# Split halves at multiples of 1024 bytes: placement in SBUF of the operands of TensorE's three-product matmuls

## The chip, the cores and the metric

One core of a Trainium2 chip. The metric is the device time of one execution in microseconds (us), the median of several runs. A lower time is better.

## The reference

Two model blocks in a row on 256 tokens of width 1024, all in float32, for one sequence:

```python
# first block, two layers
for layer in range(DEPTH):
    h = rms_norm(x, g_mix[layer])
    qkv = h @ w_in[layer]
    ...
    mix = jnp.concatenate([o_a, o_b, o_c], axis=-1)
    x = x + mix @ w_out[layer]
    h2 = rms_norm(x, g_ffn[layer])
    x = x + conv_gated_mlp(h2, w_up[layer], conv_w[layer], conv_b[layer], w_down[layer]).astype(x.dtype)
return rms_norm(x, g_final)
# second block, one layer
    xn = rmsnorm(h, norm1_g[layer])
    proj = xn @ w_in[layer]
    ...
    h = h + merged @ w_out[layer]
    hn = rmsnorm(h, norm2_g[layer])
    h = h + peer_ffn(hn, peer_wq[layer], peer_k1[layer], peer_k2[layer], peer_u[layer], peer_v[layer])
```

`o_a`, `o_b` and `o_c` are three kinds of attention. The second block has a state-space branch and an attention on chosen keys. `peer_ffn` chooses 128 of 16384 experts for each token; the kernel computes the hidden value of every expert, multiplies it by a gate that is zero for those not chosen, and sums over all.

## The kernel before

**Units.** The weights come from HBM as units of 128 partitions x 1024 floats (512 KB each), in one fixed list, `plan`. A unit goes into a slot: unit i into slot i % 6 up to the end of `keys`, and from the experts' units on (`ut`, `vt`) into slot j % 4. A slot has three buffers of 1024 words a partition: `raw`, `wh` and `wl`. SyncE issues the load of a unit into `raw` as soon as the slot's last unit has been split.

**The split.** For most products float32 accuracy is had from three matmuls of a faster type (fp32r): ScalarE copies `raw` to `wh`, rounded (line 1112); VectorE (line 1461) or GpSimd (line 2117) writes the remainder, `raw` - `wh`, to `wl`; a table `lower` says who. The activations are split the same way: `hh` and `hl`, the normed tokens turned (8 slices of 256 columns each); `yTh` and `yTl`, the hidden values of the gated MLP (22 slices of 256 columns each); `ach` and `acl`, 256 columns of the experts' gated hidden values, two buffers each. The function `mm3` issues for each pair of slices high x high, high x low and low x high (line 542), all into one PSUM bank:

```python
for j, (a, b) in enumerate(((0, 0), (0, 1), (1, 0))):
    m = p.e.matmul(out, lhs[i][a], rhs[i][b], start=start and i == 0 and j == 0, stop=stop and i == n - 1 and j == 2)
```

The second argument is the stationary operand, always 128 columns here; the third one is the moving operand. The profile writes out<-moving,stationary.

**Stages, in the order of the program,** with the products of line 542 that a unit has:

| stage | units | matmuls per unit | moving | stationary |
|---|---|---|---|---|
| win, wout (both layers) | 24 + 8 each | 12 | 512 columns of `wh`/`wl` | 128 of `hh`/`hl` |
| wup (both layers) | 44 each | 24 | 256 of `hh`/`hl` | 128 of `wh`/`wl` |
| wdown (both layers) | 22 each | 12 | 512 of `wh`/`wl` | 128 of `yTh`/`yTl` |
| wout2 | 8 | 12 | 512 of `wh`/`wl` | 128 of `hh`/`hl` |
| wpq | 16 | 24 | 256 of `hh`/`hl` | 128 of `wh`/`wl` |
| ut (experts, up) | 128 | 24 | 256 of `hh`/`hl` | 128 of `wh`/`wl` |
| vt (experts, down) | 128 | 12 | 512 of `wh`/`wl` | 128 of `ach`/`acl` |

Between the two blocks' ends stand products in whole float32 (lines 597, 837, 967, 533), straight from `raw`, which are not split. In `ut`, from unit 59 on, each unit is followed by eight small products that make the gates of four tokens; VectorE makes their one-hot operands. Before, VectorE does the routing (the choice of experts) with buffers that are cut from the upper part of `H` by `RT`, from word `R_AT` on. `H` holds the hidden values, 256 words a unit; ScalarE writes unit j of it, and from the unit on that reaches into the routing's buffers it waits for the event selG (line 1415), VectorE's last copy of routing results.

**Placement.** Each tensor of SBUF is allocated by `scoped`, one behind the other in the order of the code; closing an `ExitStack` frees its part for what comes next. In the built program the first one, `xs`, begins at byte 16512 of a partition: 16384 bytes are kept as scratch for DMAs whose descriptors GpSimd writes, and 128 hold constants. From there on follow `xs` (8192 bytes), `ids` (512), `hh` and `hl` (8192 each; `hw` and `sel_s` use the same bytes at other times), `sta` (3040), then 4 buffers each of `raw`, `wh` and `wl` (4096 each), and so on. The sizes of `sta` (760 words), `con` (1612) and `sml` (788) are what they need.

Of the kernel before, what the change touches and what calls it, by code (L numbers as in the profile page):

```python
# [30 lines left out]
K_W = K_T + 256  # L31
# [8 lines left out]
S_W = S_AIM + 16  # L40
# [55 lines left out]
def program(nc, x_d, pos_d, consts_d, smalls_d, win_d, wout_d, wup_d, wdown_d, rows_d, wu_d, wqkv_d, wqk_d, wga_d, wsm_d,  # L96
            wglu_d, wsu_d, wau_d, wout2_d, wpq_d, keys_d, ut_d, vt_d, out_d, spill_d):
    with ExitStack() as ctx:

        def scoped(where, name, n, dt=F32):  # L100
            return where.enter_context(nc.sbuf_tensor(name, [128, n], dt))

        xs = scoped(ctx, "xs", 2048)
        ids = scoped(ctx, "ids", 128)

# [1 line left out]
        hh, hl = scoped(sc_h, "hh", 2048, F32R), scoped(sc_h, "hl", 2048, F32R)  # L107
        sc_h.close()
        hw, sel_s = scoped(ctx, "hw", 2048), scoped(ctx, "sel_s", 2048)
        sta = scoped(ctx, "sta", 760)  # L110
        raws = [scoped(ctx, f"raw{i}", 1024) for i in range(4)]
        whs = [scoped(ctx, f"wh{i}", 1024, F32R) for i in range(4)]
        wls = [scoped(ctx, f"wl{i}", 1024, F32R) for i in range(4)]
        early = ExitStack()
        con_s = scoped(early, "con", K_W - 128)
        sml_s = scoped(early, "sml", S_W)
        tab_s = scoped(early, "tab", 8192)
        raws += [scoped(early, f"raw{i}", 1024) for i in (4, 5)]
        whs += [scoped(early, f"wh{i}", 1024, F32R) for i in (4, 5)]
# [34 lines left out]
        def signal(name, step=1):  # L154
            return Signal(ctx.enter_context(nc.semaphore(name)), name, step)
# [4 lines left out]
        x0_in, x1_in, pos_in, id_in, con_in, sml_in, wsb_in, wsc_in, out_sent, spilled, back_in = [  # L160
            signal(n, 16) for n in ("x0_in", "x1_in", "pos_in", "id_in", "con_in", "sml_in", "wsb_in", "wsc_in", "out_sent", "spilled", "back_in")]
# [140 lines left out]
        def sml(c, n):  # L302
            return sml_s[:, c:c + n]
# [130 lines left out]


        H = H_s[:, :].rearrange("p (j t) -> p j t", j=128)
        R_AT = 16800
        assert R_AT >= K_W - 128 + S_W + 8192 + 6144
        r_at = [R_AT]

        def RT(n):
# [653 lines left out]
        def act(a):  # L1095
            def load(out, src, sig, ev):
                a.e.dma_start(out, src).then_inc(sig.up(ev), 16)
# [63 lines left out]
            for t in range(2):  # L1161
                squares(("n", 0), t, x[:, t, :], mix[:, t, :], 0, (x0_in, x1_in)[t], "x")
            stream_up_to(first["win", 0])
            load(con_s[:, :], consts_d[:, 128:K_W], con_in, "con")
            load(sml(0, S_W), smalls_d, sml_in, "sml")
            turned(("n", 0), (0, ), 2)
            stream_up_to(first["win", 0] + 1)
# [238 lines left out]
            for j in range(128):  # L1406
# [7 lines left out]
                a.wait_ge(pe_out, ("hid", j))  # L1414
                if j * 256 + 256 > R_AT:
                    a.wait_ge(dve_out, ("selG", 1))
# [838 lines left out]
        for engine in (pe, sp, act, dve, pool):  # L2255
            engine(Engine(Count(), True))
# [8 lines left out]
        @block.scalar  # L2265
        def _(e):
            act(Engine(e, False))
# [130 lines left out]
```

## Time and profile before

| | |
|---|---|
| time, median of 3 runs | 1750.53 us (1750.17 to 1751.01) |
| span of the profiled execution | 1747.2 us |
| matmuls | 10714 |
| PE busy (union of modelled durations) | 1691.7 us, 97% |
| DVE, ACT, POOL busy | 1149.2, 821.6, 706.5 us |
| HBM read | 279.33 MB, 161 GB/s over the span |

The page gives the profiled execution by its span alone. Times inside it are us from the span's start. PE is TensorE, DVE VectorE, ACT ScalarE, POOL GpSimd, SP SyncE. A matmul's duration in a row runs from its start to a modelled end, so the durations of neighbours overlap; starts are measured. The timeline rounds to 0.01 us, and so a distance between matmuls is best taken over a whole unit: 12 distances in a stage with 512 moving columns, 24 in one with 256, or 11 where a wait stands at the unit's border.

### The profile page before, as it was taken

To read this page: it belongs to the slowest core of one execution; us is meant where nothing else is said; L and a number is where in the kernel's file an instruction comes from. 1 tells how busy PE (TensorE), PEld (TensorE's weight loads), DVE (VectorE), ACT (ScalarE), POOL (GpSimd) and SP (SyncE) were. 2 spreads that over 40 slices of the span, in tenths; PEclk is the share of its full clock that TensorE was granted. 3 is DMA by queue.
4 is the path that set the end of the run, shared out by engine and by line. 5 is a ranking of instruction groups with operands and counts; after the bars stand their busy time and mean duration, and the time that the engine had idled before them with its cause. 6 is when DMAs were issued, how large, how long until landed. Compare 5 with 4: busy or idle time off the path is not lost.

```text
span 1747.2 us, 27224 instructions
## 1 busy us (share of the span) xinstructions
PE 1691.7 (97%) x10714; PEld 1454.8 (83%) x10714; DVE 1149.2 (66%) x2422; ACT 821.6 (47%) x1453; POOL 706.5 (40%) x384
## 2 busy tenths in 40 slices
PE   7999999999999998999999999999999999999997
PEld 6779998777799986544579999999999988888885
DVE  6655785756367576666332999999999644444443
ACT  5455665354476642113243554544444455555553
POOL 2424667132357721432163999700000144444443
PEclk9999999999999999999999999999999999999998
DMA  7333545463255564323353656544444566666664
GB/s 292 112 109 132 182 162 195 150 217 108 74 193 190 173 203 134 111 87 109 95 194 134 216 167 198 179 147 145 145 140 139 160 193 193 194 194 195 195 193 134
DMA packets 77455, 283.20 MB, mean 162 GB/s; under 512 B 8720, under 2 KB 8976, under 8 KB 77072
## 3 DMA queue, kind: packets, MB, share of 16 engines
q1 hardware_dynamic: 76032, 276.50, 48.8%
q10 hardware_dynamic: 1296, 4.97, 0.8%
q8 instruction: 85, 1.39, 0.3%
q14 instruction: 42, 0.34, 0.1%
HBM read 279.33 MB, written 2.10 MB: 161 GB/s over the span
## 4 chain that ended last, share of the span: by engine, by line
PE 78%; DVE 8%; ACT 5%; POOL 5%; issue 3%; DMA 1%; POOLq 0%; DVEq 0%; ACTq 0%
PE bank L542 62%; PE bank L533 7%; PE bank L597 5%; POOL wl L2117 4%; ACT wh L1112 2%; DVE att L1478 2%; PE bank L665 1%; DVE wl L1461 1%; ACT att L1115 1%; PE bank L967 1%; PE bank L889 1%; DVE ssb L1467 1%; DVE mix L1506 1%; DVE xs L1467 1%; PE bank L837 0%
## 5 line engine op out<-in xcount | busy, mean ns | idle before, releaser
L2117 POOL TENSOR_TENSOR wl<-raw,wh 128x1024 fp32r<-128x1024 f32 x213 | 548.0, 2584 | 699.6 <-ACT wh L1112 691.1
L542 PE MATMUL bank<-hh,wh 128*128 128x256 f32 x1856 | 526.2, 284 | 5.5 <-POOL wl L2117 4.8
L1112 ACT ACTIVATE wh<-raw 128x1024 fp32r<-128x1024 f32 x476 | 492.7, 1050 | 57.2 <-PE bank L542 40.8
L542 PE MATMUL bank<-hl,wh 128*128 128x256 f32 x1856 | 519.1, 280 | 0.0
L542 PE MATMUL bank<-hh,wl 128*128 128x256 f32 x1856 | 518.1, 279 | 0.0
L1461 DVE TENSOR_TENSOR wl<-raw,wh 128x1024 fp32r<-128x1024 f32 x263 | 352.8, 1347 | 98.7 <-ACT wh L1112 98.2
L542 PEld LDWEIGHTS bank<-hh,wh 128*128 128x128 f32 x1856 | 349.1, 188 | 7.0 <-POOL wl L2117 6.0
L542 PEld LDWEIGHTS bank<-hl,wh 128*128 128x128 f32 x1856 | 349.2, 188 | 0.0
L542 PEld LDWEIGHTS bank<-hh,wl 128*128 128x128 f32 x1856 | 349.0, 188 | 0.0
L1467 DVE TENSOR_TENSOR acl<-H,ach 128x256 fp32r<-128x256 f32 x128 | 87.5, 685 | 181.6 <-ACT ach L1115 181.6
L542 PE MATMUL bank<-wh,ach 128*128 128x512 f32 x512 | 199.3, 389 | 0.4 <-DVE acl L1467 0.4
L542 PE MATMUL bank<-wh,acl 128*128 128x512 f32 x512 | 199.2, 389 | 0.0
L542 PE MATMUL bank<-wl,ach 128*128 128x512 f32 x512 | 199.2, 389 | 0.0
L1115 ACT ACTIVATE H<-bank 128x256 f32<-128x256 f32 (+32 forms) x199 | 64.7, 325 | 240.6 <-PE bank L542 208.0
L1115 ACT ACTIVATE ach<-H 128x256 fp32r<-128x256 f32 x128 | 53.4, 418 | 172.7 <-PE bank L542 172.2
L542 PE MATMUL bank<-wh,hh 128*128 128x512 f32 x288 | 119.3, 414 | 5.5 <-DVE hl L1467 2.9
L1478 DVE SCALAR_TENSOR_TENSOR att<-bank,sml,att 128x255 f32<-128x255 f32 (+1 forms) x176 | 84.4, 480 | 56.7 <-ACT att L1115 53.5
L542 PE MATMUL bank<-wh,hl 128*128 128x512 f32 x288 | 114.1, 396 | 0.0
L542 PE MATMUL bank<-wl,hh 128*128 128x512 f32 x288 | 113.9, 396 | 0.0
L542 PEld LDWEIGHTS bank<-wh,ach 128*128 128x128 f32 x512 | 96.1, 188 | 20.7 <-issue 0.6
L542 PEld LDWEIGHTS bank<-wh,acl 128*128 128x128 f32 x512 | 96.1, 188 | 20.0
L542 PEld LDWEIGHTS bank<-wl,ach 128*128 128x128 f32 x512 | 96.1, 188 | 19.7
(216 smaller groups left out, 2313.4 us busy)
## 6 DMA issues: line engine op xcount, KB each, us to landing
raw<-in_ut_dram SPq DMA_DIRECT2D x128, 512.0 KB, 3.5
raw<-in_vt_dram SPq DMA_DIRECT2D x128, 512.0 KB, 3.8
raw<-in_wup_dram SPq DMA_DIRECT2D x88, 512.0 KB, 4.2
raw<-in_win_dram SPq DMA_DIRECT2D x48, 512.0 KB, 4.6
raw<-in_wdown_dram SPq DMA_DIRECT2D x44, 512.0 KB, 4.2
raw<-in_wout_dram SPq DMA_DIRECT2D x24, 512.0 KB, 3.6
raw<-in_wga_dram SPq DMA_DIRECT2D x16, 512.0 KB, 3.6
raw<-in_wpq_dram SPq DMA_DIRECT2D x16, 512.0 KB, 5.1
```

What stands on the lines that cost most here:

```text
L533: m = p.e.matmul(out, l, r, start=i == 0, stop=i == len(pairs) - 1)
L542: m = p.e.matmul(out, lhs[i][a], rhs[i][b], start=start and i == 0 and j == 0, stop=stop and i == n - 1 and j == 2)
L597: m = p.e.matmul(banks[b][:, 0:cw], whole[:, off + h * kper + k, tcols(t)], unit_whole(i, k, kper, slice(0, cw)), start=h == 0 and k == 0, ...
L665: m = p.e.transpose(banks[b][:, 256 * (i % 2) + 128 * k:256 * (i % 2) + 128 * k + 128], buf[:, o:o + 128], ids[:, :])
L889: s = p.e.matmul(banks[yb][o:o + 32, 0:256], l[:, 32 * n:32 * n + 32], turned_z[n % 2][:, a, b, :], start=j == 0, stop=j == 3, tile_positi ...
L967: m = p.e.matmul(banks[b][:, :], hTw[:, 2 * h + k, tcols(t)], unit_whole(i, k, 2, slice(0, 512)), start=h + k == 0, stop=h + k == 2)
L1112: a.e.activation(high_of(u), raw_of(u), ACTF.Copy).then_inc(act_hi.up(("hi", u)), 1)
L1115: a.e.activation(out, src, f, **kw).then_inc(act_out.up(ev), 1)
L1461: v.e.tensor_tensor(low_of(u), raw_of(u), high_of(u).bitcast(F32), ALU.subtract).then_inc(dve_lo.up(("lo", u)), 1)
L1467: v.e.tensor_tensor(out, a, b, op).then_inc(dve_out.up(ev), 1)
L1478: v.e.scalar_tensor_tensor(out, a, s, b, op0, op1).then_inc(dve_out.up(ev), 1)
L2117: g.e.tensor_tensor(low_of(u), raw_of(u), high_of(u).bitcast(F32), ALU.subtract).then_inc(pool_lo.up(("lo", u)), 1)
```

## The change

```diff
@@ -100,6 +100,7 @@
+        scoped(ctx, "pad0", 96)
         xs = scoped(ctx, "xs", 2048)
         ids = scoped(ctx, "ids", 128)
@@ -107,13 +108,13 @@
         hh, hl = scoped(sc_h, "hh", 2048, F32R), scoped(sc_h, "hl", 2048, F32R)
         sc_h.close()
         hw, sel_s = scoped(ctx, "hw", 2048), scoped(ctx, "sel_s", 2048)
-        sta = scoped(ctx, "sta", 760)
+        sta = scoped(ctx, "sta", 768)
...
-        con_s = scoped(early, "con", K_W - 128)
-        sml_s = scoped(early, "sml", S_W)
+        con_s = scoped(early, "con", 1664)
+        sml_s = scoped(early, "sml", 896)
@@ -434,8 +435,8 @@
-        R_AT = 16800
-        assert R_AT >= K_W - 128 + S_W + 8192 + 6144
+        R_AT = 16896
+        assert R_AT >= 1664 + 896 + 8192 + 6144
@@ -1161,7 +1162,7 @@
-            load(con_s[:, :], consts_d[:, 128:K_W], con_in, "con")
+            load(con_s[:, 0:K_W - 128], consts_d[:, 128:K_W], con_in, "con")
@@ -2383,7 +2384,7 @@
-    nc = _bacc.Bacc("TRN2", target_bir_lowering=False, num_devices=1)
+    nc = _bacc.Bacc("TRN2", target_bir_lowering=False, num_devices=1, dynamic_dma_scratch_size=1024)
```

The scratch for GpSimd's DMAs shrinks from 16384 to 1024 bytes a partition, a pad of 96 words stands in front, and three small buffers are rounded up. What that does to the start of each buffer in a partition, by the addresses in the two built programs:

| buffer | before, byte | modulo 1024 | after, byte | modulo 1024 |
|---|---|---|---|---|
| `xs` | 16512 | 128 | 1536 | 512 |
| `ids` | 24704 | 128 | 9728 | 512 |
| `hh`, `hw` | 25216 | 640 | 10240 | 0 |
| `hl`, `sel_s` | 33408 | 640 | 18432 | 0 |
| `raw0` to `raw3` | 44640 and on | 608 | 29696 and on | 0 |
| `wh0` to `wh3` | 61024 and on | 608 | 46080 and on | 0 |
| `wl0` to `wl3` | 77408 and on | 608 | 62464 and on | 0 |
| `raw4`, `raw5`, `wh4`, `wh5`, `wl4`, `wl5` | 136192 and on | 0 | 121856 and on | 0 |
| `yTh`, `yTl` | 183296, 205824 | 0 | 168960, 191488 | 0 |
| `H` | 93792 | 608 | 78848 | 0 |
| `ach`, `acl` | 224864 and on | 608 | 209920 and on | 0 |

A moving slice is 1024 bytes (256 columns) or 2048 bytes (512), a stationary one 512 bytes, so stationary slices lie at the buffer's offset or 512 bytes behind it.

The instructions are the same but for one wait. `H`'s unit j reaches past `R_AT` when 256 j + 256 is larger: from j = 65 on with 16800, from j = 66 on with 16896. On ScalarE's engine in ut, where unit 65 is copied out of its bank (`H<-bank 128x232`, with 24 columns that stay in the bank), stood before:

```order
L1115 ACTIVATE H<-bank 128x63x4 [waits pe_out]
L1112 ACTIVATE wh<-raw 128x1024 [waits slot0_in]
L1115 ACTIVATE H<-bank 128x232 [waits dve_out,pe_out]
L1115 ACTIVATE bank<-bank 128x24
L1115 ACTIVATE H<-bank 128x62x4 [waits pe_out]
L1112 ACTIVATE wh<-raw 128x1024 [waits slot1_in]
L1115 ACTIVATE H<-bank 128x228 [waits pe_out]
```

and now, with the lines one further down:

```order
L1116 ACTIVATE H<-bank 128x63x4 [waits pe_out]
L1113 ACTIVATE wh<-raw 128x1024 [waits slot0_in]
L1116 ACTIVATE H<-bank 128x232 [waits pe_out]
L1116 ACTIVATE bank<-bank 128x24
L1116 ACTIVATE H<-bank 128x62x4 [waits pe_out]
L1113 ACTIVATE wh<-raw 128x1024 [waits slot1_in]
L1116 ACTIVATE H<-bank 128x228 [waits dve_out,pe_out]
```

The wait for VectorE (dve_out, the event selG) has moved from unit 65 to unit 66, one unit later.

## Rows read from the trace of the kernel before

**Rows 1.** the chain of waits, shares of the span by line
```profile
by line: PE bank L542 61.6%; PE bank L533 7.4%; PE bank L597 4.8%; POOL wl L2117 3.9%; issue 3.5%; ACT wh L1112 2.2%; DVE att L1478 1.7%; PE bank L665 1.1%; DVE wl L1461 1.1%; ACT att L1115 0.9%; PE bank L967 0.8%; PE bank L889 0.8%; DVE ss
```

**Rows 2.** the page's 40 slices: VectorE's busy tenths, TensorE's granted clock
```profile
DVE  6655785756367576666332999999999644444443
...
PEclk9999999999999999999999999999999999999998
```

**Rows 3.** groups by form, line 542: columns as in the page's part 5
```profile
L542 PE MATMUL bank<-hh,wh 128*128 128x256 f32 x1856 | 526.2, 284 | 5.5 <-POOL wl L2117 4.8 <-DVE hl L1467 0.8
...
L542 PE MATMUL bank<-wh,ach 128*128 128x512 f32 x512 | 199.3, 389 | 0.4 <-DVE acl L1467 0.4
...
L542 PE MATMUL bank<-wh,hh 128*128 128x512 f32 x288 | 119.3, 414 | 5.5 <-DVE hl L1467 2.9 <-POOL wl L2117 2.4
...
L542 PE MATMUL bank<-wh,yl 128*128 128x512 f32 x176 | 69.6, 395 | 0.0
```

**Rows 4.** timeline of TensorE in vt, one unit apart: start, duration in us
```profile
1600.20 0.39 PE L542 MATMUL bank<-wh,ach 128*128 128x512 f32 x1
...
1602.92 0.39 PE L542 MATMUL bank<-wh,ach 128*128 128x512 f32 x1
```

**Rows 5.** timeline of TensorE in wdown, layer 1, starts of units
```profile
631.43 0.39 PE L542 MATMUL bank<-wh,yh 128*128 128x512 f32 x1
...
634.15 0.40 PE L542 MATMUL bank<-wh,yh 128*128 128x512 f32 x1
...
636.96 0.39 PE L542 MATMUL bank<-wh,yh 128*128 128x512 f32 x1
...
645.36 0.40 PE L542 MATMUL bank<-wh,yh 128*128 128x512 f32 x1
...
648.12 0.39 PE L542 MATMUL bank<-wh,yh 128*128 128x512 f32 x1
```

**Rows 6.** timeline of TensorE in win, layer 1, units in slots 2 and 4
```profile
355.06 0.40 PE L542 MATMUL bank<-wh,hh 128*128 128x512 f32 x1
...
357.62 0.40 PE L542 MATMUL bank<-wh,hl 128*128 128x512 f32 x1
...
360.65 0.39 PE L542 MATMUL bank<-wh,hh 128*128 128x512 f32 x1
...
363.22 0.40 PE L542 MATMUL bank<-wh,hl 128*128 128x512 f32 x1
```

**Rows 7.** timeline of TensorE in ut, one unit apart
```profile
989.84 0.28 PE L542 MATMUL bank<-hh,wh 128*128 128x256 f32 x1
...
992.64 0.28 PE L542 MATMUL bank<-hh,wh 128*128 128x256 f32 x1
```

**Rows 8.** timeline of TensorE in wup, layer 1, starts of units
```profile
549.67 0.28 PE L542 MATMUL bank<-hh,wh 128*128 128x256 f32 x1
...
560.98 0.29 PE L542 MATMUL bank<-hh,wh 128*128 128x256 f32 x1
...
566.68 0.28 PE L542 MATMUL bank<-hh,wh 128*128 128x256 f32 x1
```

**Rows 9.** timeline of TensorE in the second block, whole-fp32 products
```profile
689.01 14.00 PE L597 MATMUL bank<-raw,hw 128*128 128x512 f32 x32
...
702.95 0.92 PE L533 MATMUL bank<-uT,BT 32*128 32x256 f32 x6
...
705.86 3.72 PE L837 MATMUL bank<-hw,raw 128*128 128x256 f32 x16
...
709.42 7.03 PE L597 MATMUL bank<-raw,hw 128*128 128x512 f32 x16
```

**Rows 10.** timeline of VectorE and ScalarE around selG
```profile
1130.65 0.93 DVE L1483 COPY xs<-bank 128x128 f32<-128x128 f32 x3
...
1158.98 0.36 ACT L1115 ACTIVATE H<-bank 128x232 f32<-128x232 f32 x1 [1.48 <-PE bank L542]
```


## The prediction

> **What bounds the kernel now.** I read the chain of waits first. It puts 61.6% of the span on one line, the three-product matmuls of line 542, all other TensorE lines far below it [rows 1]. TensorE's clock is granted at 9 tenths or more almost throughout, which is the 2.4 GHz level, so 256 columns at one per cycle would take 106.7 ns and 512 would take 213.3 ns [rows 2]. The busy shares are of no use here: a row's mean (280 ns for 256 columns) is the latency of one matmul, and neighbours overlap. What counts is the distance from one matmul's start to the next, which the timeline shows, and how many there are: 3 x 1856 with 256 moving columns, 3 x (512 + 288 + 176) with 512 [rows 3].
>
> Now the placements, as offsets modulo 1024, moving buffer first, then stationary. In rows the order is the same: out <- moving, stationary. The timeline has a unit of twelve 512-column matmuls in five placements:
> - vt, 608 with 608: 1600.20 to 1602.92, 2.72 us, 226.7 ns each [rows 4].
> - wdown in slot 5, 0 with 0: 631.43 to 634.15, again 2.72 us. In slots 0 to 3, 608 with 0: from 634.15, 2.81 us for slot 0 (entering from slot 5), then 8.40 us for the three units of slots 1 to 3, 2.80 us or 233.3 ns each. Slot 4, 0 with 0 but entered from slot 3: 2.76 us [rows 5].
> - win in slot 2, 608 with 640: eleven distances in 2.56 us, 233 ns. In slot 4, 0 with 640: eleven in 2.57 us, 233 ns [rows 6].
>
> So neither buffer's own offset decides, but the two together: equal offsets give 226.7 ns, at 608 as at 0, unequal ones 233 ns, and the state carries over for a few matmuls. The change makes all of them 0 with 0 (stationary slices 0 or 512, as y's are now), which is what slot 5 of wdown has already. This is a comparison inside one execution, with the same engines at work beside it.
>
> For 256 columns every unit is 24 matmuls and the moving buffer is at 640. In ut (stationary 608) a unit takes 2.80 us, 116.7 ns each [rows 7]. In wup, four units of slots 0 to 3 (608) take 11.31 us, 117.8 ns each, and the two of slots 4 and 5 (stationary at 0) take 5.70 us, 118.75 ns each [rows 8]. Nothing in the trace has 256 columns with 0 and 0.
>
> **The change part by part.** It adds and removes no instruction; each term is a number of matmuls by a change of distance, on TensorE, which is the end's own path.
> - wdown: six units (one turn of the slots) take 16.69 us [rows 5], at 2.72 us each 16.32 us. 0.37 us for each six, 44 units: **-2.7 us**.
> - win, wout and wout2: 3 x 288 matmuls make 72 units, each with some ten unbroken distances (the eleventh often holds a wait or another product, which stays). 72 x 10 x 6.4 ns: **-4.6 us** [rows 3, 6].
> - wup and wpq: 88 + 16 units. Six units take 17.01 us [rows 8]. The new distance I take as 116.7 ns, 16.80 us for six: 0.21 us for each six, 3.6 us; the first few units of a stage already run lower, so **-3.4 us**.
> - ut: 128 units at 2.80 us stay so: **0**. vt: 128 units at 2.72 us: **0**, it has equal offsets now.
> - The unknown is thus the 256-column distance with 0 and 0. Bounds: from below the whole-fp32 products, which take two passes and fetch the same bytes more slowly. 16 of 256 columns start from 705.86 to 709.42, 222.5 ns or 111 ns a pass; 32 of 512 from 689.01 to 702.95, 435.6 ns or 218 ns a pass [rows 9]. From above 120 ns, the 13.3 ns that an in-step 512-column matmul has over 213.3, put on 106.7. I take 116.7 because it is the lowest distance that the same kind of matmul shows over whole units, and ut holds it for most of its length. One nanosecond is worth 5568 x 1 ns = 5.6 us.
> - The wait of ScalarE on selG moves from hidden unit 65 to 66. VectorE's three copies that release it begin at 1130.65, ScalarE's unit 65 starts at 1158.98 and waits for TensorE [rows 10]. 28 us of cover: nothing. Were it gone, one wait of under 1 us.
> - `sta`, `con` and `sml` grow and the stretch used for routing moves up by 96 words in H: no element count changes, **0**. No DMA of this program is issued by GpSimd, so the smaller scratch has no user: 0. The cover is that there is nothing to issue from it.
> - The whole-fp32 products keep their distances: **0**. At 435.6 ns for two passes they are within 2% of 426.7, so at most some tenths of a microsecond for each stage could come.
>
> What is late next: in wup and wdown the splits on VectorE and GpSimd are ahead of TensorE, which starts back to back there; a unit that is 1 to 3% shorter leaves that so.
>
> Two rules stand beside this. The trace shows vt at 226.7 ns, wdown slots 1 to 3 at 233.3 with the same moving offset and another stationary one [rows 4, 5]. The Trainium skill, "SBUF — State Buffer", section "Who interferes with whom", says that TensorE has one read port for moving data and an independent one for weight loads, and that TensorE never waits on anyone. By that rule the place of the stationary buffer could not matter and the sum would be 0; the rows disagree. And rows 9 show whole-fp32 passes of 218 ns. The skill's "TensorE: Matmul & The Clock Gate", section "Back-to-back issue gap", gives columns / 2.4 + 2.5 ns for matmuls in a row, 215.8 for 512 and 109.2 for 256. An estimate by it would be some 86 us less than now, if aligned buffers reached it; slot 5, aligned in both, stands at 226.7.
>
> Sum: -2.7 - 4.6 - 3.4 = **-10.7 us**. The profiled span of 1747.2 us would become 1736.5. The runs' median is 1750.5, 3.3 us above the span; the difference lies outside it and stays. Forecast **1739.8 us**.
>
> **The rivals.**
> - **A, faster.** If the overhead in step is in proportion to the columns (13.3 ns for 512, so 6.7 for 256), the 256-column distance becomes 113.3 ns and a unit 2.72 us. For it: the unequal distances halve exactly (233.3 for 512 and 116.7 for 256), so 256 columns may be out of step now. Against it: ut's distance is steady, as an in-step one would be. wup and wpq gain 104 x 0.08 = 8.3 us more. In ut 128 x 0.08 = 10.2 us would be on offer, but VectorE is at 9 tenths or more for its second half [rows 2] and GpSimd makes the low halves in the first, so I count half. 1739.8 - 8.3 - 5 = 1726; with all of it 1721.
> - **B, slower.** If the overhead in step is a fixed 13.3 ns for each load of the stationary operand, 256 columns go to 120.0 ns, a unit to 2.88 us. For it: slots 4 and 5 of wup, whose stationary halves lie at 0, are the slowest [rows 8]. Place: ut, 128 x 0.08 = 10.2 us; wup and wpq, 104 x 0.045 = 4.7 us. Less the 7.3 us of the 512-column stages: +7.6, 1758. The mean of all 232 units is 2.816 us now (128 at 2.80, 104 at 17.01 / 6), 117.3 ns a matmul. B decides from 2.847 us a unit on, 118.6 ns, where it eats the 7.3 us, and is visible from 119.3.
> - **C, no effect.** The distances differ for another reason that goes with the slot (which engine writes beside it, high address bits), or the allocator places something otherwise. Against it: slots 1 to 3 agree to 10 ns and vt has equal offsets and the low distance. 1750.5.
> - **D, down to the whole-fp32 pass.** 218 and 111 ns: (226.7 - 218) x 1536 + (233 - 218) x 1392 + (117.3 - 111) x 5568 = 13 + 21 + 35 = 69 us, 1681. wdown slot 5 speaks against it.
>
> **How the numbers follow.** Forecast 0.50, A 0.25, B 0.10, C 0.12, D 0.03. The likeliest gives 1739.8, by itself 1736 to 1744 (10.7 us, give or take a third). The range must leave out no more than 0.2. Up to 1751 it takes in C; down to 1722 it takes in the forecast and A as far as its share in ut is half paid or a little more, some 0.20 of its 0.25. Left out are B, D and A in full, 0.18. A measurement of this kernel tells 0.2%, 3.5 us, from no change. Faster by more: forecast, A and D, 0.78. Within: C, 0.12. Slower: B, 0.10.
>
> **What would show it.** In the changed profile: all units of wdown 2.72 us, slots 0 to 3 as slot 5; eleven distances in win 2.49 us; wup 2.80 us whatever the slot; ut 2.80 and vt 2.72 as now; ACT, DVE and GpSimd rows as before. A ut unit of 2.72 us is A, of 2.88 us B. wdown's slots still at 2.80 is C. The prediction is wrong if 512-column distances with 0 and 0 are not 226.7 ns where the stationary operand is hh, or if 256-column ones leave 116.7.

## The result

| | before | after |
|---|---|---|
| time, median | 1750.57 us (1748.95 to 1751.91, 6 runs) | 1756.84 us (1755.06 to 1757.04, 6 runs) |
| span of the profiled execution | 1747.2 us | 1755.2 us |
| ratio | | 1.0036, 95% interval 1.0024 to 1.0047 |

The change makes the kernel slower by 6.3 us. The forecast was 1739.8 us, the range ended at 1751. Rival B had said 1758, with 120.0 ns for each 256-column matmul.

The chain of waits of the changed kernel (lines are one further down, L542 is now L543), by engine and by line; before, line 542 had 61.6% [rows 1]:

```profile
PE 87%; DVE 4%; POOL 4%; ACT 2%; DMA 1%; issue 1%; SPq 0%; POOLq 0%; ACTq 0%; DVEq 0%
PE bank L543 70%; PE bank L534 8%; PE bank L598 5%; POOL wl L2118 3%; PE bank L666 1%; PE bank L890 1%; ACT wh L1113 1%; PE bank L968 1%; PE bank L838 1%; DVE ssb L1468 1%; DVE xs L1468 1%; DMA raw<-in_win_dram 0%; DVE mix L1507 0%; POOL ssv L2123 0%; DVE wl L1462 0%
```

Its costliest groups, columns as in the profile's part 5, which answer to [rows 3]:

```profile
L543 PE MATMUL bank<-hh,wh 128*128 128x256 f32 x1856 | 531.3, 286 | 4.1 <-POOL wl L2118 3.2
...
L543 PE MATMUL bank<-wh,ach 128*128 128x512 f32 x512 | 199.3, 389 | 0.4 <-DVE acl L1468 0.4
...
L543 PE MATMUL bank<-wh,hh 128*128 128x512 f32 x288 | 118.0, 410 | 6.8 <-POOL wl L2118 3.3
```

A mean of 286 ns in place of 284 is a latency and says nothing. The starts do: the distance from one matmul's start to the next is what a matmul costs here. TensorE's timeline of the changed kernel, start and duration in us, each pair a unit or several apart:

```profile
353.42 0.39 PE L543 MATMUL bank<-wh,hh 128*128 128x512 f32 x1
...
355.92 0.39 PE L543 MATMUL bank<-wh,hl 128*128 128x512 f32 x1
...
373.20 0.48 PE L543 MATMUL bank<-wh,hh 128*128 128x512 f32 x1
...
375.83 0.39 PE L543 MATMUL bank<-wh,hl 128*128 128x512 f32 x1
...
548.14 0.28 PE L543 MATMUL bank<-hh,wh 128*128 128x256 f32 x1
...
565.42 0.28 PE L543 MATMUL bank<-hh,wh 128*128 128x256 f32 x1
...
616.97 0.39 PE L543 MATMUL bank<-wh,yh 128*128 128x512 f32 x1
...
633.29 0.39 PE L543 MATMUL bank<-wh,yh 128*128 128x512 f32 x1
...
987.14 0.28 PE L543 MATMUL bank<-hh,wh 128*128 128x256 f32 x1
...
990.02 0.28 PE L543 MATMUL bank<-hh,wh 128*128 128x256 f32 x1
...
1612.42 0.39 PE L543 MATMUL bank<-wh,ach 128*128 128x512 f32 x1
...
1615.14 0.39 PE L543 MATMUL bank<-wh,ach 128*128 128x512 f32 x1
```

- wup, six units from 548.14 to 565.42: 17.28 us, 2.88 each or **120.0 ns** a matmul; before 17.01 [rows 8].
- ut, one unit from 987.14: 2.88 us, **120.0 ns**; before 2.80 [rows 7].
- wdown, six units from 616.97 to 633.29, all slots: 16.32 us, 2.72 each or **226.7 ns**; before 16.69 [rows 5].
- win, eleven distances from 353.42: 2.50 us, 227 ns; before 2.56 [rows 6]. But 373.20 to 375.83, a unit behind a pause, takes 2.63 us.
- vt, one unit from 1612.42: 2.72 us, as before [rows 4].

So 512 columns behave as forecast, 256 columns as rival B said. Where the 8.0 us of span went, from the first to the last matmul of line 542 (543) in each stage; the means are over the distances inside runs, without pauses, and are read from the trace's own time stamps, which are finer than the timeline's 0.01 us:

| stage | before, us | after, us | difference | mean distance before, after, ns |
|---|---|---|---|---|
| win and wout, both layers, wout2 | 297.92 | 295.72 | -2.2 | 233.0, 229.1 |
| wup, both layers | 249.12 | 253.36 | +4.2 | 118.0, 120.0 |
| wdown, both layers | 123.87 | 119.47 | -4.4 | 232.1, 226.8 |
| wpq and ut | 475.35 | 483.49 | +8.1 | 116.9, 119.8 |
| vt | 348.09 | 348.09 | 0.0 | 226.7, 226.7 |
| middle: end of wdown to wout2 | 202.81 | 204.84 | +2.0 | none |
| the other borders | | | +0.3 | |

The 2.0 us of the middle, in which no split half is multiplied, are not the addresses' doing: an experiment below with the addresses of before (`before_late`) has 204.62 there, and two with `hh` at 0 (`m1` and `m2`) have 202.91, as short as before. Executions of one kernel differ by that much: the span of 1747.2 us belongs to an execution of about 1749 us, the lowest of before's six, and the changed kernel's profiled execution, 1757.04 us, is the highest of its six. The medians differ by 6.3 us, about the 8.0 less the 2.0 of the middle.

### The profile page after: what moved, and what is told of

Read it like the earlier page. It is cut to its first block, busy times and chain, and to the rows that moved or that the text cites. A ratio compares the mean times of both kernels' runs of the same rounds, so it can differ in the third digit from the quotient of the medians.

```text
span 1755.2 us, 27224 instructions
## 1 busy us (share of the span) xinstructions
PE 1701.8 (97%) x10714; PEld 1469.2 (84%) x10714; DVE 1148.0 (65%) x2422; ACT 822.8 (47%) x1453; POOL 708.1 (40%) x384
## 4 chain that ended last, share of the span: by engine, by line
PE 87%; DVE 4%; POOL 4%; ACT 2%; DMA 1%; issue 1%; SPq 0%; POOLq 0%; ACTq 0%; DVEq 0%
PE bank L543 70%; PE bank L534 8%; PE bank L598 5%; POOL wl L2118 3%; PE bank L666 1%; PE bank L890 1%; ACT wh L1113 1%; PE bank L968 1%; PE bank L838 1%; DVE ssb L1468 1%; DVE xs L1468 1%; DMA raw<-in_win_dram 0%; DVE mix L1507 0%; POOL ssv L2123 0%; DVE wl L1462 0%
## 5 line engine op out<-in xcount | busy, mean ns | idle before, releaser
L543 PE MATMUL bank<-hh,wh 128*128 128x256 f32 x1856 | 531.3, 286 | 4.1 <-POOL wl L2118 3.2
L543 PE MATMUL bank<-hh,wl 128*128 128x256 f32 x1856 | 525.1, 283 | 0.0
L543 PE MATMUL bank<-hl,wh 128*128 128x256 f32 x1856 | 525.0, 283 | 0.0
L543 PEld LDWEIGHTS bank<-hh,wh 128*128 128x128 f32 x1856 | 355.8, 192 | 5.1 <-POOL wl L2118 4.1
L543 PEld LDWEIGHTS bank<-hl,wh 128*128 128x128 f32 x1856 | 356.1, 192 | 0.0
L543 PEld LDWEIGHTS bank<-hh,wl 128*128 128x128 f32 x1856 | 355.7, 192 | 0.0
L543 PE MATMUL bank<-wh,ach 128*128 128x512 f32 x512 | 199.3, 389 | 0.4 <-DVE acl L1468 0.4
L543 PE MATMUL bank<-wh,acl 128*128 128x512 f32 x512 | 199.2, 389 | 0.0
L543 PE MATMUL bank<-wl,ach 128*128 128x512 f32 x512 | 199.2, 389 | 0.0
L543 PE MATMUL bank<-wh,hh 128*128 128x512 f32 x288 | 118.0, 410 | 6.8 <-POOL wl L2118 3.3
L543 PEld LDWEIGHTS bank<-wh,ach 128*128 128x128 f32 x512 | 96.1, 188 | 20.7 <-issue 0.6
L543 PE MATMUL bank<-wh,hl 128*128 128x512 f32 x288 | 112.9, 392 | 0.0
L543 PEld LDWEIGHTS bank<-wl,ach 128*128 128x128 f32 x512 | 96.1, 188 | 19.9
L543 PEld LDWEIGHTS bank<-wh,acl 128*128 128x128 f32 x512 | 96.1, 188 | 19.9
L543 PE MATMUL bank<-wl,hh 128*128 128x512 f32 x288 | 112.5, 391 | 0.0
```

## The experiments

The theories, from the first reading of the changed trace. **R**: only the difference between the moving and the stationary operand's place counts, and the same difference is good for 512 columns and bad for 256. **N**: multiples of 1024 are themselves bad for 256 columns. **S**: it hangs on the slot, through what other engines write there. All kernels of this part but one (`before_late`, below) are the changed kernel, with a helper that pads in front of a buffer, and six constants. `hw` and `sel_s` move with `hh` and `hl`, and the word at which the routing's buffers start is computed from the sizes. The code is cut to what matters:

```diff
+        def placed(where, name, n, off, dt=F32):
+            pad_to(where, off)          # up to the next address that is off modulo 1024
+            return scoped(where, name, n, dt)
...
-        hh, hl = scoped(sc_h, "hh", 2048, F32R), scoped(sc_h, "hl", 2048, F32R)
+        hh, hl = placed(sc_h, "hh", 2048, OFF_H, F32R), placed(sc_h, "hl", 2048, OFF_HL, F32R)
...
-        whs = [scoped(ctx, f"wh{i}", 1024, F32R) for i in range(4)]
+        whs = [placed(ctx, f"wh{i}", 1024, OFF_W[i], F32R) for i in range(4)]
```

and the same for wl (OFF_WL), y (OFF_Y) and ach, acl (OFF_A). What is not named is at 0, as in the change.

### Everything at 608

```diff
+        OFF_H, OFF_HL, OFF_W, OFF_WL, OFF_Y, OFF_A = 608, 608, (608,) * 6, (608,) * 6, 608, 608
```

> Every split half (hh, hl, wh, wl, y, ach, acl) at byte 608 modulo 1024 instead of 0, all else as in the changed kernel. Theory R (only the difference between the moving and the stationary offset counts; at equal offsets each weight load costs a fixed 13.3 ns): a wup or ut unit of 24 stays 2.88 us (120.0 ns a matmul), wdown and vt units 2.72 us, time as the changed kernel's, 1757 give or take 2. Theory N (it is the multiple of 1024 itself that costs with 256 columns): 2.80 us or so, time 1740.

1756.81 us in one execution, beside 1749 for before. TensorE in ut, one unit apart: 2.88 us.

```profile
986.98 0.28 PE L560 MATMUL bank<-hh,wh 128*128 128x256 f32 x1
...
989.86 0.28 PE L560 MATMUL bank<-hh,wh 128*128 128x256 f32 x1
```

All stages are as in the changed kernel, to 0.3 us. N falls: 608 with 608 is as bad as 0 with 0 for 256 columns, and as good for 512.

### hh and hl 32 bytes further on

```diff
+        OFF_H, OFF_HL = 32, 32
```

> The changed kernel with hh and hl alone moved 32 bytes up (32 modulo 1024), the difference that most units had before. Theory R: 256-column units back to between 2.80 and 2.83 us (116.7 to 117.8 ns) in every slot, win and wout out of step again at 233 ns, wdown and vt 226.7 ns. Against before the wdown gain of 2.7 us and about 2 to 3 us of slots 4 and 5 remain: 1745, between 1743 and 1747. Theory N: hh is no longer on a multiple of 1024, so also faster than 1757, but nothing says 116.7. Theory S (the slot, or what is written beside it, sets the distance and not the placement): 1757 again.

1747.50 us, ratio to before 0.9987 (0.9978 to 0.9996). TensorE in wup, six units apart, and in ut, one unit apart:

```profile
549.27 0.28 PE L560 MATMUL bank<-hh,wh 128*128 128x256 f32 x1
...
566.08 0.28 PE L560 MATMUL bank<-hh,wh 128*128 128x256 f32 x1
...
987.96 0.28 PE L560 MATMUL bank<-hh,wh 128*128 128x256 f32 x1
...
990.75 0.28 PE L560 MATMUL bank<-hh,wh 128*128 128x256 f32 x1
```

16.81 us for six units of layer 1's wup (116.7 ns) and 2.79 for one of ut (116.7 by the trace's own stamps). wdown and vt, whose operands did not move, stay at 226.6 and 226.7 ns, win goes back to 233.3. wpq, with the same difference of 32 bytes, ran at 117.8 ns throughout. By the two ratios, 0.9987 and 1.0036, the 32 bytes between the operands are worth 0.49% or 8.6 us against the changed kernel: its whole loss, and more. The 1745 expected was somewhat too low.

Layer 0's wup shows a limit to the price of a nanosecond. It took 124.6 us here, as in before with 118.0 ns: from its unit 37 on TensorE waits for splits, 1.4 us in all, and these waits give the gain back. The kernels below that have `hh` at 64 or 960 and the same offsets in every slot take 124.1 to 124.6 us there too, even at 113.3 ns a matmul.

### Two maps: each slot at another offset

```diff
+        OFF_W = OFF_WL = (0, 32, 64, 128, 256, 512)        # first map
+        OFF_W = OFF_WL = (992, 960, 896, 96, 928, 768)     # second map
```

> A map: hh, hl, y, ach at 0; wh and wl of slots 0 to 5 at 0, 32, 64, 128, 256, 512 modulo 1024. Theory R: the distance follows the slot's offset. 256 columns (wup, wpq six slots, ut four): slot 0 120.0 ns, slot 3 (128) 118 to 119; if the offsets count modulo 512, slot 5 is 120.0 like slot 0. 512 columns (win, wdown six slots, vt four): slot 0 226.7, slots 1 to 3 about 233, slot 5 226.7. Theory S: all slots alike, 120.0 and 226.7.

> The same map with slots 0 to 5 at 992, 960, 896, 96, 928, 768 modulo 1024, that is the moving hh lies 32, 64, 128, 928, 96, 256 above the stationary wh. Theory R: slot 0 (as before's slots 0 to 3) 116.7 to 117.8 ns with 256 columns, slot 2 (as before's slots 4, 5) 118.75; 512 columns about 233 in slots 0 to 4. Some difference may do better than 116.7 with 256 columns. Theory S: all slots alike, 120.0 and 226.7.

vt in the first map, starts of units in slots 0, 1, 2, 3 and 0:

```profile
1612.25 0.39 PE L560 MATMUL bank<-wh,ach 128*128 128x512 f32 x1
...
1614.97 0.40 PE L560 MATMUL bank<-wh,ach 128*128 128x512 f32 x1
...
1617.78 0.40 PE L560 MATMUL bank<-wh,ach 128*128 128x512 f32 x1
...
1620.54 0.39 PE L560 MATMUL bank<-wh,ach 128*128 128x512 f32 x1
...
1623.32 0.39 PE L560 MATMUL bank<-wh,ach 128*128 128x512 f32 x1
```

2.72, 2.81, 2.76 and 2.78 us, by the trace's own stamps 226.6, 233.4, 228.5 and 232.1 ns where a unit has settled. Both maps together, by the difference of moving minus stationary offset, in ns:

| difference, bytes | 256 columns (wup, wpq, ut) | 512 columns (wdown, vt, win) |
|---|---|---|
| 0, 256, 512 (also -256) | 120.0 | 226.7 |
| +32 | 116.7 (the wpq above: 117.8) | 233.4 |
| -32 | 118.3 | 232.4 to 233.6 |
| +64 | 117.8, in some units 113.3 | 228.5 |
| -64 | 117.7, in some units 113.4 | 233.4 |
| 128 | 118.8 | 232 |
| +96 | 120.2 | 234 |
| -96 | 117.6 | 234 to 235 |

R stands, with a period that no row of before had shown: 256 bytes, since 256, 512 and -256 read as 0. S falls: slot 4 at 256 and slot 5 at 512 read as slot 0 at 0. (A slot's first matmuls still carry the last slot's spacing, so a value of a mixed kernel may be off by half a ns.)

The table fits before's rows, modulo 256. ut is 640 - 608 = +32: 116.7 [rows 7]. wup's slots 0 to 3 have +32 as well, and ran at 117.8, in turn with slots 4 and 5 [rows 8], so +32 has two levels, of which a run of matmuls keeps one. wup's slots 4 and 5 are 640 - 0, which is 128: 118.8 [rows 8]. wdown's slots 0 to 3 are 608 - 0, +96: 233 to 234 [rows 5]. win's slot 2 is 608 - 640, -32: 233 [rows 6]. The kernel before had, by chance, a good difference for 256 columns in its longest 256-column stage; of the eight tried, only 64 bytes has a lower level.

### hh and hl 64 bytes after and 64 bytes ahead

```diff
+        OFF_H, OFF_HL = 64, 64
+        OFF_H, OFF_HL = 960, 960
```

> The changed kernel with hh and hl 64 bytes up: with 256 columns the moving operand lies 64 above the stationary one in every slot, in win and wout 64 below. In the maps that difference gave 117.8 ns where the unit before lay otherwise, and 113.3 ns in units that began after a pause. Theory R with memory (what state a unit is in follows from the one before, and a pause starts it afresh): with one difference everywhere the 113.3 ns last, a ut unit is 2.72 us, and 5568 matmuls save up to 3.3 ns each against 116.7; win at 233.4 ns. About 1732, down to 1728. If the low state is not lasting: 117.8 ns and 1750.

> The changed kernel with hh and hl at 960 modulo 1024, 64 below the stationary halves with 256 columns and 64 above the moving ones' counterpart in win and wout. The maps gave 117.7 or 113.4 ns with 256 columns, and 228.5 ns with 512 columns for this sign, against 233.4 for the other. Theory R with memory: ut units 2.72 us as with h64, win and wout 228.5 to 229, so some 3 us under h64: 1729, down to 1725. If the low state is not lasting: 117.7 ns, 1747.

64: 1751.14 us, 1.0009 (1.0000 to 1.0018); 117.8 ns in layer 1's wup and mostly in ut. 960: **1744.03 us, 0.9958 (0.9945 to 0.9972)**, faster than both kernels, though neither comes near the 1732 and 1729 that were hoped for. There ut has two levels; TensorE, one unit apart at 987.66 and at 1078.60:

```profile
987.66 0.28 PE L560 MATMUL bank<-hh,wh 128*128 128x256 f32 x1
...
990.38 0.28 PE L560 MATMUL bank<-hh,wh 128*128 128x256 f32 x1
...
1078.60 0.28 PE L560 MATMUL bank<-hh,wh 128*128 128x256 f32 x1
...
1081.43 0.28 PE L560 MATMUL bank<-hh,wh 128*128 128x256 f32 x1
```

2.72 us (113.3 ns) and 2.83 (117.8), with the same buffers, the same code and 1.0 of the clock. A unit hands its level to the next one where there is no pause between them (all 44 units of layer 1's wup stand at 117.8), and after a pause it can be the other one: after the pause ahead of unit 30 the distances begin 201, 118, 117, 118 and stay at 117.8 for 25 units; where they begin, as in unit 28, with a falling row (124, 118, 113) they stay at 113.3. So a level is a property of the run of matmuls, not of one matmul.

### Four maps for a lasting low level

```diff
+        OFF_H, OFF_HL, OFF_W, OFF_WL = 960, 960, (0,) * 6, (32, 64, 128, 192, 224, 96)      # m5
+        OFF_H, OFF_HL, OFF_W, OFF_WL = 960, 0, (0,) * 6, (0, 32, 960, 128, 224, 96)         # m6
+        OFF_H, OFF_HL = 960, 64;  OFF_W = OFF_WL = (0, 128, 32, 160, 64, 192)               # m7
+        OFF_H, OFF_HL = 960, 896; OFF_W = OFF_WL = (0, 128, 160, 224, 64, 192)              # m8
```

> A map: hh and hl at 960, all wh at 0, and the low halves wl of the six slots at 32, 64, 128, 192, 224 and 96 (modulo 1024). With hh and hl at 960 and all at 0, the 256-column distance has two levels, 113.3 and 117.8 ns, and a unit picks one at its start and hands it on. R (the difference of moving and stationary operand of each matmul counts): a third of a unit's matmuls (stationary wl) now has another difference than the other two thirds, so a unit has a mixed mean between 113.3 and 120, and the slots differ: 64 (same as two turns of 64) and 192 should show other means than 224. If the memory of the level is in the run of matmuls and not in each one, some slot sends every unit to the low level: units at 113.3 in that slot throughout. If only the stationary operand's first half counts, or wh alone, all slots read as with all at 0: 113.3 or 117.8. vt (moving wh and wl, stationary ach and acl at 0): wh against 0 is equal, wl unequal, so 226.7 to 233 by slot. Whole: 1742 to 1762 us.

> A map: hh at 960, hl at 0, all wh at 0, and wl of the six slots at 0, 32, 960, 128, 224 and 96 (modulo 1024). In the 256-column stages one third of the matmuls (moving hl, stationary wh) is then at equal offsets. R: those alone would be at 120.0 ns; a unit of slot 0 has a mean of about 118 (two thirds at 117.8 or 113.3, one at 120.0), 115.5 if the low level holds, and 120.0 if equal ones set the pace for their neighbours. A change of difference inside a run of matmuls could also restart the low level each time: then 113.3 throughout in some slot. Whole: 1742 to 1762 us.

> A map: hh at 960, hl at 64 and both halves of a slot at 0, 128, 32, 160, 64 and 192 (modulo 1024). In the map before, the one slot in which every unit of wup, wpq and the first half of ut ran at 113.3 ns had differences moving minus stationary of -64, -64 and +64 (modulo 256) for the three products. If what keeps the low level is that differences of -64 and +64 take turns, slot 0 (-64, +64, -64) or slot 1 (+64, -64, +64) is at 113.3 throughout, and this can be had with both halves of all slots at one offset, so that the 512-column stages stay in step. If the low level needs the stationary halves themselves apart, both slots read 117 to 119. Slot 4 (-128, 0, -128) 118 to 120. Whole: 1745 to 1762 us, since four slots are bad ones.

> A map like the last one with hl 64 below hh instead of 128 above: hh 960, hl 896, slots at 0, 128, 160, 224, 64, 192. Differences by slot: (-64, -128, -64), (+64, 0, +64), (+32, -32, +32), (-32, -96, -32), (-128, +64, -128), (0, -64, 0), modulo 256. Looked for is a slot with 113.3 throughout; if only turns of -64 and +64 give it, none shows here, and all read 116.6 to 120. Whole: 1750 to 1762 us.

In m5 slot 2 (wl 128 bytes behind wh's offset) ran at 113.4 ns in every unit of wup, wpq and ut, its neighbours at 117.7 to 118.9. In the second half of ut, where gate products stand between the units, TensorE in unit 82 (slot 2) and unit 83 (slot 3, wl at 192), eighteen matmuls apart in each:

```profile
1220.60 0.28 PE L560 MATMUL bank<-hh,wh 128*128 128x256 f32 x1
...
1222.64 0.28 PE L560 MATMUL bank<-hh,wh 128*128 128x256 f32 x1
...
1224.23 0.28 PE L560 MATMUL bank<-hh,wh 128*128 128x256 f32 x1
...
1226.35 0.28 PE L560 MATMUL bank<-hh,wh 128*128 128x256 f32 x1
```

2.04 us or 113.3 ns, and 2.12 us or 117.8. m6, m7 and m8 had no slot below 117.5. So turns of -64 and +64 as such don't do it (m7's slots 0 and 1 have them too, at 117.6 and 117.7). What else slot 2 of m5 has is that its stationary halves lie 128 bytes apart; m6's slot 3 has that too, with another hl, at 117.9.

### The low level everywhere

The low half of a slot is written and read 128 bytes further on where it is stationary, and at 0 where it moves, so that wdown and vt keep equal offsets. hh and hl are at 960.

```diff
-        wls = [placed(ctx, f"wl{i}", 1024, OFF_WL[i], F32R) for i in range(4)]
+        wls = [placed(ctx, f"wl{i}", 1056, OFF_WL[i], F32R) for i in range(4)]
...
+        STAT = [(first["wup", L], 44) for L in range(DEPTH)] + [(first["wpq"], first["vt"] - first["wpq"])]
...
         def low_of(i):
-            return wls[slot[i]][:, 0:plan[i][1]]
+            v = 32 if any(a <= i < a + n for a, n in STAT) else 0
+            return wls[slot[i]][:, v:v + plan[i][1]]
```

> hh and hl at 960, all halves of the slots at 0, but where a slot is the stationary operand (wup, wpq, ut) its low half is written and read 128 bytes further on (buffers of 1056 words), which gives the differences -64, -64, +64 that held 113.3 ns in one slot of the map. wdown and vt keep everything at 0. If the differences of the run of matmuls set the level: wup, wpq and the first 59 units of ut at 113.3 ns, wdown and vt at 226.7. Against the kernel with hh and hl at 960 alone (1744.03): wup of layer 1 about 44 x 24 x 4.5 ns = 4.7 us less, wpq 1.7, ut units 30 to 54 some 2.7, together 9, less what the second half of ut gives back (118.8 in the map for this slot, 5 us at most): 1735 to 1740 us. If the map's low slot owed its level to its neighbours with other differences, 117 to 118 everywhere and 1745 to 1750 us.

A second kernel takes 48 words in place of 32 from unit 59 of ut on:

> The same, and from unit 59 of ut on, where small gate products stand between the units, the low half 192 bytes further on (differences -64, -64, 0), which was the slot at 113.3 ns there in the map. If that carries over: units 59 to 127 of ut at 113.3 ns in place of 117.8 to 118.8, some 69 x 24 x 5 ns = 8 us less than the kernel with one shift if VectorE and GpSimd keep up, 1729 to 1736 us; if the neighbours made it, as that kernel.

The first has 113.3 ns in every unit of wup, wpq and all of ut once it has settled, 226.7 in wdown and vt, and measured 1749.17 us, 0.9994 (0.9985 to 1.0003): no gain where 1735 to 1740 was expected. The second has 117.8 ns from unit 59 on and measured 1752.0, 1.0011 (1.0002 to 1.0020). Its expectation gives the low level of m5's second half of ut to the slot at 192 bytes. It was the slot at 128 that had it there too (units 82 and 83 above); the one at 192 stood at 117.8, and the second kernel shows the same. In the first kernel wup of layer 1 took 3.8 us less than in the kernel at 960, of which pauses in the next six units of wdown gave back 2.6. From the start of unit 27 of ut to that of unit 59 it took 108.5 us where the kernel at 960 has 95.8 and before 92.5: there the gain went. TensorE:

```profile
1039.06 0.28 PE L563 MATMUL bank<-hh,wl 128*128 128x256 f32 x1
1047.88 0.90 PE L1071 MATMUL bank<-ids,H 128*128 128x128 f32 x3 [8.55 <-DVE H L1488]
1048.44 0.56 PE L563 MATMUL bank<-hh,wh 128*128 128x256 f32 x1
1048.80 0.41 PE L563 MATMUL bank<-hl,wh 128*128 128x256 f32 x1
1049.01 0.41 PE L563 MATMUL bank<-hh,wl 128*128 128x256 f32 x1
...
1079.52 0.28 PE L563 MATMUL bank<-hh,wh 128*128 128x256 f32 x1
...
1082.24 0.28 PE L563 MATMUL bank<-hh,wh 128*128 128x256 f32 x1
```

Unit 30's turn of the choice (L1071) starts 8.55 us after TensorE ran dry, released by VectorE's L1488 (9.4 us from the last matmul of unit 29 to the first of unit 30), and the next matmuls come 213 ns apart. There is a second such pause of 4.8 us ahead of unit 57, behind which all of that unit's matmuls come over 200 ns apart. Units themselves take 2.72 us, as from 1079.52. The windows just before, in and behind the pause, columns as the first line says:

```profile
core 0: us, PE busy (x) PEld busy (x) DVE busy (x) ACT busy (x) POOL busy (x), PEclk, DMA share, GB/s
1030.00:1039.00 9.00, 8.38 (x74) 8.19 (x73) 8.93 (x3) 4.12 (x6) 9.00 (x3) 1.00 0.50 167
1039.40:1047.80 8.40, 0.00 (x0) 0.00 (x0) 8.23 (x4) 1.42 (x2) 8.28 (x4) 0.76 0.57 170
1048.40:1050.40 2.00, 2.00 (x11) 2.00 (x10) 1.83 (x9) 0.00 (x0) 0.00 (x0) 0.50 0.77 207
1050.80:1055.00 4.20, 4.20 (x39) 4.20 (x38) 3.80 (x19) 1.33 (x2) 1.07 (x1) 1.00 0.02 4
```

The granted clock fell from 1.00 to 0.50 (from 2.4 to 1.2 GHz) across the pause and was back at 1.00 by 1050.8. What VectorE did in the pause, and GpSimd:

```profile
1038.48 2.29 DVE L1512 TENSOR_REDUCE H<-H 128x128 f32<-128x2048 f32 x1
1041.19 0.20 DVE L1508 RECIPROCAL H<-H 128x8 f32<-128x8 f32 x1
1041.43 6.40 DVE L1488 TENSOR_TENSOR H<-H 128x128 f32<-128x128 f32 x1
```
```profile
1022.49 25.19 POOL L2138 TENSOR_TENSOR wl<-raw,wh 128x1024 fp32r<-128x1024 f32 x8 [1.92 <-ACT wh L1133]
1053.93 2.43 POOL L2138 TENSOR_TENSOR wl<-raw,wh 128x1024 fp32r<-128x1024 f32 x1 [6.25 <-ACT wh L1133]
```

A multiply of 128x128 elements took 6.40 us, and ended when GpSimd's unbroken run of eight splits did (1022.49 + 25.19 = 1047.68). In before it took 1.75 us, beside splits that follow one another without a gap as well:

```profile
1041.92 1.75 DVE L1467 TENSOR_TENSOR H<-H 128x128 f32<-128x128 f32 x1
```

### The routing's marks later

```diff
-        J_SEL = (25, 51)
-        J_TURN = (30, 57)
-        J_GATE, N_GR = 59, 64
+        J_SEL = (28, 55)
+        J_TURN = (33, 61)
+        J_GATE, N_GR = 63, 64
```

> The kernel with one shifted view (differences -64, -64, +64 in wup, wpq and ut), and the routing's marks in ut moved: the two choices' last steps from units 25 and 51 to 28 and 55, the two turns of the selection on TensorE from 30 and 57 to 33 and 61, the first gate products from unit 59 to 63. In the kernel with the old marks TensorE ran at 113.3 ns but stood 9.4 us ahead of unit 30 and 4.8 us ahead of unit 57, each time until VectorE had finished its choice, and started again at half the clock (213 ns each). If that is where the gain went: both pauses gone or under 3 us, distances 113.3 throughout ut, some 13 us less than 1749.2: 1734 to 1740 us. If VectorE is behind by more than the three or four units give (some 8 to 11 us of matmuls), the second turn still waits: 1740 to 1746. If the gain is lost elsewhere (splits, gates at VectorE's pace in the second half): 1747 to 1751.

> The kernel before with the same later marks, and its own addresses. There the pauses ahead of units 30 and 57 are short (about 0.4 us and below), so later marks should give nothing: 1748 to 1753 us, ratio 0.999 to 1.001. If the later marks were a gain by themselves (two pauses of 1.6 us before the turns, at the last steps of the choices, go away), 1747 to 1748.

`J_SEL` and `J_TURN` name the units of ut beside which the routing's steps stand; `J_GATE` is the first unit with gate products, and up to it GpSimd makes the low halves, so it now makes four more.

With the shifted view: **1736.18 us (1734.76 to 1745.42), 0.9928 (0.9910 to 0.9946)**. On the kernel before: 1750.55, 1.0001 (0.9992 to 1.0010), so the marks alone are worth nothing. This is where the low distance of 256 columns is paid out. How much of it the kernel at 960 with the later marks, without the shifted view, would have reached was not run. Two of six executions stood at 1744 and 1745, the other four at 1734.8 to 1736.2; the profiled one was of the former, and in it the small multiply took 13.65 us.

### GpSimd breaks off once

```diff
+                        if u == first["ut"] + 32:
+                            g.wait_ge(dve_out, ("picked", 0))
                         g.e.tensor_tensor(low_of(u), raw_of(u), high_of(u).bitcast(F32), ALU.subtract)
```

> The kernel with one shifted view and later marks, and GpSimd waits with its split of unit 32 of ut until VectorE's last multiply of the first choice (picked, 0) has been done. In the profiled execution without this wait that multiply, 128x128 elements, began at 1042.90 and took 13.65 us (1.75 us in before), up to the end of an unbroken run of 11 of GpSimd's splits, and TensorE stood 5.9 us ahead of unit 33. Theory G: the multiply can't get in between GpSimd's splits. Then it takes under 2.5 us here, GpSimd stands still for some tenths of a us, TensorE has no pause ahead of unit 33, and all executions lie at or below the faster ones without the wait: 1733 to 1737 us, none at 1744. Rival V: VectorE is late by its own work, the long multiply is an artefact of the record. Then TensorE waits as before and some executions stay at 1744 to 1745.

> The same wait in the kernel with one shifted view and the old marks. There the multiply began at 1041.43 and took 6.40 us, and TensorE stood 8.8 us ahead of unit 30. G: it takes about 2 us, ends near 1043.3, TensorE's pause becomes 4 to 5 us: 4 to 5 us less than 1749.2, about 1745. The rest of the pause is VectorE's own lateness, which only the later marks take away (late_gap). V: no change, 1747 to 1751.

Later marks with the wait: 1741.32 us (1736.23 to 1745.13), 0.9958 (0.9944 to 0.9972). VectorE and GpSimd in its profiled execution:

```profile
1043.28 1.83 DVE L1488 TENSOR_TENSOR H<-H 128x128 f32<-128x128 f32 x1
```
```profile
1022.70 22.26 POOL L2140 TENSOR_TENSOR wl<-raw,wh 128x1024 fp32r<-128x1024 f32 x6 [0.29 <-ACT wh L1133]
1045.25 16.79 POOL L2140 TENSOR_TENSOR wl<-raw,wh 128x1024 fp32r<-128x1024 f32 x7 [0.29 <-DVE H L1488]
```

The multiply took 1.83 us, GpSimd resumed 0.14 us after its end, and TensorE has no pause over 0.4 us ahead of unit 33: G's mechanism at this place. All three profiled executions with the shifted view and without the wait have the long multiply (6.40, 6.40 and 13.65 us), both with the wait have it under 2 us. G's forecast of the times failed: executions up to 1745 remain, as V had said, and the median is not below the 1736.18 without the wait. With the old marks, 1741.81 (1739.86 to 1749.54), 0.9952 (0.9938 to 0.9965), better than the 1745 expected. Its profiled execution, the slowest at 1749.54, has the multiply at 1.81 us and the pause ahead of unit 30 cut from 9.4 to 4.8 us, but the pause ahead of unit 57, 4.8 us without the wait, is 9.3 us, and there another VectorE operation took 14.02 us beside GpSimd's splits:

```profile
1111.52 14.02 DVE L1488 TENSOR_TENSOR H<-H,sta 128x2048 f32<-128x2048 f32 x1
```

Others of 128x2048 take 4.4 us beside GpSimd's splits, and 2.29 us where GpSimd is idle. So it isn't that one multiply: other VectorE operations with two SBUF inputs can be kept out too, and which one was differed between the profiled executions. That the unprofiled executions at 1741 to 1745 have such a case too is argued, not shown.

The Trainium skill, "SBUF — State Buffer", section "Who interferes with whom", has VectorE and GpSimd share one port pair as an exclusive lock, under which the one that issues second blocks until the first has finished, and counts among the cases a VectorE instruction with two SBUF inputs beside a GpSimd instruction that reads SBUF. The trace agrees that VectorE gets no further while a split runs: the 1.75 us multiply of before ended 0.14 us after a split did (1043.53). But the 6.40, 13.65 and 14.02 us reach over the ends of two to five of GpSimd's splits. What lets VectorE in at the first end in one execution and not in another stays open. VectorE's two-input operations of over 5 us stand in all five profiled executions with the shifted view, and in none of the other thirteen; whether TensorE's pace or the shifted place of the low halves brings them on, no run tells apart.

## Why the prediction failed, step by step

- **The failed step** is "I take 116.7 because it is the lowest distance that the same kind of matmul shows over whole units". No row had 256 columns at equal offsets; there the distance is 120.0 ns. The prediction had seen for 512 columns that the two offsets together decide, equal being best, and took the same order over to 256 columns. It is the other way round: equal is nearly the worst of the eight differences tried. By its own price of 5.6 us a ns, 3.3 ns are 18 us; against what stood there before the loss is 12.3 us (4.2 in wup, 8.1 in wpq and ut), as wup and wpq came from 118.
- **wup and wpq**, forecast -3.4: measured +4.2 for wup and +0.8 for wpq.
- **ut**, forecast 0: +7.3. 128 units at 0.08 us would be 10.2. In wpq and ut together the pauses for GpSimd's splits are 1.6 us shorter (3.2 for 4.8), so of the net +8.1 us the distances make up some 9.7. A slower TensorE waits less for its splits.
- **wdown**, forecast -2.7: the distances gave -2.8, right, in all slots as in slot 5. Another -1.6 came from one pause of 1.72 us for a split in layer 0's wdown that is gone; the forecast had no such pause.
- **win, wout, wout2**, forecast -4.6: -2.2. The sign and the settled distance (226.7) were right; the size was off since these stages are full of short waits, behind each of which the distances take up to nine matmuls to settle (in the unit at 373.20: 235, 234, 236, 224, 231, 235, 229, 232, 231, then 227 ns), so the mean is 229.1. The 6.4 ns were 3.9.
- **vt**, forecast 0: 0.0. **selG's wait, pads, scratch, DMA, whole fp32**, forecast 0: nothing of them shows; the 2.0 us of the middle come with before's addresses too. That whole fp32 takes two passes is the prediction's reading of 435.6 ns, which is 2.04 times 213.3; no run shows passes.
- **From span to time**: the prediction took 1750.5 less 1747.2, 3.3 us, as lying outside the span. Only 1.8 us do (1757.04 beside 1755.2); the rest is that the profiled execution was one of the short ones. It moves the forecast by 1.5 us and did not decide.
- **B** was right in mechanism as far as the numbers go (13.3 ns on 106.7 and on 213.3 alike) and in size: 1758 against 1756.8, or +7.6 against the +6.3 of the medians. That its sum agrees with the 8.0 us of the spans is in part luck: ut gave 2.9 us less than its 10.2, and the middle 2.0 us that belong to no address. It was held back to 0.10 because slots 4 and 5 of wup were its only support. They were not at equal offsets but at 128, so they did not support it; that no row spoke against B should have given it more than that. A fixed cost for each load of the stationary operand is not shown either: +96 has 120.2 ns without equal offsets.
- The 215.8 and 109.2 ns that the prediction takes from the Trainium skill, "TensorE: Matmul & The Clock Gate", section "Back-to-back issue gap", stand there for an isolated matmul. Nothing in its sum rests on them; the lowest settled distances here are 226.7 and 113.3 ns.
- **A**'s 113.3 ns exist, but at a difference of 64 bytes, not at 0. Its caveat was sound: pauses for VectorE and GpSimd took back in ut what TensorE gained.

## What to carry to other kernels

For fp32r matmuls of these two shapes that follow one another without a wait, choose the place of the moving operand relative to the stationary one, modulo 256 bytes, and per shape: with 512 columns equal offsets (226.7 ns against 233.4), with 256 columns not equal ones (120.0 against 116.7 at +32, and 113.3 at -64 with the low stationary half 128 bytes off). A buffer that serves both shapes can be read through two views. Where no row shows a combination, a rule that holds for another shape is no estimate of it; one cheap run of the smallest edit (32 bytes) would have been. And when TensorE gets faster, look at what paces it next: here layer 0's wup gained next to nothing below 118 ns, and the rest came only after the routing's marks had moved.

## What was not expected of the hardware

- The period of 256 bytes in the difference, and the opposite order for 256 and 512 columns.
- Two levels, 113.3 and 117.8 ns, for the same instructions on the same buffers, kept over up to 44 units and sometimes changed by a pause. Why is open; nothing here looks inside TensorE's reads.
- A VectorE multiply of 128x128 elements that took 1.75 us in one kernel took 6.40 and 13.65 in others, where TensorE uses a unit in 2.72 us in place of 2.80 and the low halves lie 128 bytes further on.
- A pause of 8.55 us of TensorE with the clock at 0.50 of full speed behind it, which cost nine matmuls 100 ns each.
